# A two-block transformer step on one core: first modulation rows in another order, shift added out of PSUM, constants and gains loaded in parts

## The reference, cut to what matters

```python
mod = silu(c) @ ada_w + ada_b                 # 9 rows of 1024: sh1, sc1, g1, sh2, sc2, g2, sh3, sc3, g3
y = rmsnorm(x, ffn1_pre_g) * (1 + sc1) + sh1
y = (silu(y @ w_gate) * (y @ w_up)) @ w_down  # 1024 -> 2816 -> 1024
h = x + 0.5 * g1 * rmsnorm(y, ffn1_post_g)
# then: a mixer of mLSTM and HGRN2 heads, a second FFN, a second block with
# attention, an RWKV recurrence and a retrieval over 16384 experts
```

## Time and profile before

| | us |
|---|---|
| median of 3 runs | 1949.12 (1948.37 to 1952.76) |
| the profiled execution | 1958.65 |
| its span in the trace | 1956.8 |
| start of the first FFN matmul in it | 53.58 |
| TensorE busy in the span | 1811.9 (93%) |

### The profile page before, as it was taken

The page is one execution under the profiler, slowest core; times in us unless marked ns, Lnnn a source line. Parts: engine busy times, 40 slices in busy tenths (PEclk is TensorE's granted clock), DMA queues, the critical chain, the costliest instruction groups (busy, mean ns, idle before and its releaser), DMA issues.

```text
span 1956.8 us, 32839 instructions
## 1 busy us (share of the span) xinstructions
PE 1811.9 (93%) x12830; PEld 1557.4 (80%) x12830; DVE 1139.4 (58%) x1952; ACT 768.4 (39%) x1170; POOL 334.8 (17%) x314
## 2 busy tenths in 40 slices
PE   4999998987899999999878899999999999999997
PEld 1777877864399978976863798999999998888885
DVE  2443545759355544695443469958889964444444
ACT  2333344451345444552111443444444443333334
POOL 1000000000000000000000038760000025555553
PEclk8999997999999998999998899999999999999999
DMA  9566554521555553442003335554444456666664
GB/s 359 208 257 245 170 178 178 185 86 66 225 172 189 176 172 119 151 151 87 3 2 129 130 123 164 179 162 140 142 141 142 145 175 192 193 192 192 193 191 158
DMA packets 62080, 315.98 MB, mean 161 GB/s; under 512 B 6896, under 2 KB 7184, under 8 KB 40720
## 3 DMA queue, kind: packets, MB, share of 16 engines
q1 hardware_dynamic: 60768, 305.94, 46.8%
q10 hardware_dynamic: 1136, 8.39, 1.2%
q0 software_dynamic: 64, 0.04, 0.0%
HBM read 313.29 MB, written 1.05 MB: 161 GB/s over the span
## 4 chain that ended last, share of the span: by engine, by line
PE 76%; DVE 9%; DMA 7%; ACT 4%; POOL 2%; issue 2%; SPq 0%; POOLq 0%; DVEq 0%; ACTq 0%
PE bank L375 21%; PE bank L376 20%; PE bank L377 20%; DMA ring<-in_stream 4%; PE bank L590 3%; DMA ring<-in_experts 2%; PE bank L2127 2%; DVE ring_rounded L353 2%; POOL ring_rounded L2419 2%; PE bank L536 2%; ACT arena_rounded L342 1%; PE bank L641 1%; DVE field L1320 1%; ACT ring_rounded L2225 1%; PE bank L1549 1%
## 5 line engine op out<-in xcount | busy, mean ns | idle before, releaser
L377 PE MATMUL bank<-yb_rounded,ring_rounded 128*128 128x256 f32 x2080 | 595.3, 286 | 0.0
L377 PEld LDWEIGHTS bank<-yb_rounded,ring_rounded 128*128 128x128 f32 x2080 | 406.0, 195 | 0.0
L353 DVE TENSOR_TENSOR ring_rounded<-ring,arena_rounded 128x1024 fp32r<-128x1024 f32 x218 | 256.9, 1221 | 218.7 <-ACT arena_rounded L342 218.4
L2225 ACT CAST ring_rounded<-ring 128x1024 fp32r<-128x1024 f32 x250 | 262.6, 1051 | 279.1 <-DMA ring<-in_experts 279.1
L375 PE MATMUL bank<-yb_rounded,arena_rounded 128*128 128x256 f32 x1104 | 323.5, 293 | 24.1 <-POOL ring_rounded L831 10.2
L376 PE MATMUL bank<-yT_rounded,arena_rounded 128*128 128x256 f32 x1104 | 319.7, 290 | 0.0
L342 ACT CAST arena_rounded<-ring 128x1024 fp32r<-128x1024 f32 x222 | 221.3, 1047 | 191.3 <-PE bank L375 119.6
L375 PE MATMUL bank<-yb_rounded,ring_rounded 128*128 128x256 f32 x976 | 283.0, 290 | 10.3 <-POOL ring_rounded L2419 7.9
L376 PE MATMUL bank<-yT_rounded,ring_rounded 128*128 128x256 f32 x976 | 275.9, 283 | 0.0
L2378 DVE TENSOR_TENSOR ring_rounded<-ring,ring_rounded 128x1024 fp32r<-128x1024 f32 x128 | 156.9, 1226 | 191.6 <-ACT ring_rounded L2225 191.6
L376 PE MATMUL bank<-ring_rounded,arena_rounded 128*128 128x512 f32 x688 | 268.4, 390 | 0.0
(11 more groups left out here) (389 smaller groups left out, 2606.1 us busy)
## 6 DMA issues: line engine op xcount, KB each, us to landing
ring<-in_stream SPq DMA_DIRECT2D x160, 1024.0 KB, 4.9
ring<-in_experts SPq DMA_DIRECT2D x256, 512.0 KB, 3.5
field<-in_gains ACTq DMA_DIRECT2D x1, 2560.0 KB, 8.9
const<-in_const SPq DMA_DIRECT2D x1, 1602.0 KB, 15.1
field<-in_gains ACTq DMA_DIRECT2D x1, 1536.0 KB, 6.7
xh<-in_x ACTq DMA_DIRECT2D x1, 1024.0 KB, 5.5
field<-in_norms ACTq DMA_DIRECT2D x1, 1024.0 KB, 10.3
field<-in_lns ACTq DMA_DIRECT2D x1, 1024.0 KB, 4.7
```

The source lines that it names most:

```text
L353: ins = nc.vector.tensor_tensor(ring_r[:, g % SLOTS, half], ring[:, g % SLOTS, half], top.bitcast(F32), ALU.subtract)
L377: return first, pe.matmul(bank, s_rest, m_top, start=False, stop=stop)
L2225: nc.scalar.copy(expert_top[:, n % E_SLOTS, :], expert_w[:, n % E_SLOTS, :]).then_inc(expert_top_ready, 1)
```

## The change

The row tiles are made in the order 2, 3, 0, 1 (`sc1` ahead of `sh1`). The bias matmul of a tile comes first in its bank, ahead of the wait for the tile's first chunk. The sum of a tile is issued between the two chunks of the next. DVE forms the scale row and multiplies both halves of the tokens while the shift tiles are computed. The sums of the shift tiles go to a `V` bank, and DVE adds them from there, times 1/32, to the 512 columns of each token half. Each such piece (two per column half) is transposed at once. Both transposes of the first column half stand in TensorE's queue ahead of the last row chunk. The ACT copies and DVE subtractions of the pieces are interleaved to match, with DVE's split of the first FFN chunk behind the last shift piece. SP loads 256 columns of `const` at the beginning and the rest ahead of chunk 20, the fourth round's first FFN tile. The load of five gain rows becomes two on ACT's queue, one row after round g = 1 and four rows after round g = 3.

```diff
+        V_seen, V_end, chunk_at, split_base = {}, {}, {"ffn1": 2 * 4}, {}
         silu_c = tiny[:, 0:KT * 32].rearrange("p (k n) -> p k n", k=KT)
         ADA, ADA_FIRST = N_MOD * D // 512, 4
+        FIRST_ROWS = [2, 3, 0, 1]
...
+        def first_rows_pe(pe, bank, tile, c):
+            if c == 0:
+                pe.matmul(bank[0:32, :], ones_32, arena1[:, tile * 512:(tile + 1) * 512], start=True, stop=False)
+            w = next_chunk(pe)[:, :].rearrange("p (k n) -> p k n", k=4)
+            for k in range(4):
+                ins = pe.matmul(bank[32 * k:32 * k + 32, :], silu_c[:, 4 * c + k, :], w[:, k, :],
+                                start=(c == 0 and k > 0), stop=(c == 1))
+                if k == 0:
+                    ins.then_inc(begun, 1)
+            if c == 1:
+                ins.then_inc(A.done, 1)
+        def first_sum_pe(pe, bank, tile, queue=A):
+            pe.matmul(bank[:, :], cst("ones"), partial(tile), start=True, stop=True).then_inc(queue.done, 1)
+        def first_turn_pe(pe, bank, i):
+            t, k = i % 2, i // 2 * 4
+            pe.wait_ge(sem("y_ffn1"), i + 1)
+            for j in range(4):
+                ins = pe.transpose(bank[:, j * P:(j + 1) * P], yb[:, t, (k + j) * P:(k + j + 1) * P], ident)
+            ins.then_inc(V.done, 1)
...
-            if tile in (0, ADA_FIRST):
-                pe.wait_ge(sem(f"ada_b_in{int(tile > 0)}"), 16)
+            if tile == ADA_FIRST:
+                pe.wait_ge(sem("ada_b_in1"), 16)
...
         def ada_pe(pe):
             pe.wait_ge(sem("silu_c_spread"), 1)
-            for tile in range(ADA_FIRST):
-                ada_groups_pe(pe, tile)
-                if tile == 0:
-                    pe.wait_ge(sem("const_in"), 16)
-                else:
-                    ada_sum_pe(pe, tile - 1, but=1)
-            ada_sum_pe(pe, ADA_FIRST - 1)
+            pe.wait_ge(sem("ada_b_in0"), 16)
+            sc_a, sc_b, sh_a, sh_b = FIRST_ROWS
+            rows = A.take(pe)
+            first_rows_pe(pe, rows, sc_a, 0)
+            first_rows_pe(pe, rows, sc_a, 1)
+            pe.wait_ge(sem("const_in"), 16)
+            for last, tile in ((sc_a, sc_b), (sc_b, sh_a)):
+                total, rows = A.take(pe), A.take(pe)
+                first_rows_pe(pe, rows, tile, 0)
+                A.evacuated_but(pe, 2)
+                first_sum_pe(pe, total, last)
+                first_rows_pe(pe, rows, tile, 1)
+            rows = A.take(pe)
+            first_rows_pe(pe, rows, sh_b, 0)
+            A.evacuated_but(pe, 1)
+            first_sum_pe(pe, V.take(pe), sh_a, V)
+            for i in range(2):
+                first_turn_pe(pe, V.take(pe), i)
+            first_rows_pe(pe, rows, sh_b, 1)
+            A.evacuated(pe)
+            first_sum_pe(pe, V.take(pe), sh_b, V)
+            for i in range(2, 4):
+                first_turn_pe(pe, V.take(pe), i)
+            V.evacuated(pe)
+        def first_turn_act(act, i):
+            t, k = i % 2, i // 2 * 4
+            act.wait_ge(V.done, FIRST_TURNS[i] + 1)
+            bank = V.banks[FIRST_TURNS[i] % 4]
+            nc.scalar.copy(y_top[:, t, k:k + 4, :], bank[:, :].rearrange("p (j s) -> p j s", j=4)
+                           ).then_inc(sem("y_top_ready"), 1)
...
-            for tile in range(ADA_FIRST):
+            for tile in FIRST_ROWS[:2]:
                 ada_groups_act(act, tile)
-                if tile:
-                    ada_sum_act(act, tile - 1)
-            ada_sum_act(act, ADA_FIRST - 1)
-            marks["first_rows"] = (A.free, 4 + A.emptied.n)
+                ada_sum_act(act, tile)
+                mark(f"row{tile}", A.free, 4 + A.emptied.n)
+            ada_groups_act(act, FIRST_ROWS[2])
+            for i in range(2):
+                first_turn_act(act, i)
+            ada_groups_act(act, FIRST_ROWS[3])
+            first_top_act(act, "ffn", "ffn1")
+            for i in range(2, 4):
+                first_turn_act(act, i)
...
-            dve.wait_ge(*marks["first_rows"])
             dve.wait_ge(sem("first_gain_in"), 16)
-            v(nc.vector.scalar_tensor_tensor(mod[:, SC1, :], mod[:, SC1, :], 1.0, gains[:, 0, :], ALU.add, ALU.mult))
+            for n, tile in enumerate(FIRST_ROWS[:2]):
+                at = slice(n * 512, (n + 1) * 512)
+                await_mark(dve, f"row{tile}")
+                ins = nc.vector.scalar_tensor_tensor(mod[:, SC1, at], mod[:, SC1, at], 1.0, gains[:, 0, at], ALU.add, ALU.mult)
+            v(ins)
+            for t in range(TT):
+                scaled_dve(t, SC1)
+            for n in range(2):
+                bank = V.get(dve)
+                at = slice(n * 512, (n + 1) * 512)
+                for t in range(TT):
+                    ins = nc.vector.scalar_tensor_tensor(yb[:, t, at], bank[:, :], 1.0 / 32, yb[:, t, at], ALU.mult, ALU.add
+                                                         ).then_inc(sem("y_ffn1"), 1)
+                dve.wait_ge(sem("y_ffn1"), 2 * n + 2)
+                nc.vector.memset(small[:, 510:511], 0.0).then_inc(V.free, 1)
+                if n == 1:
+                    first_rest_dve(dve, "ffn", "ffn1")
+                for i in (2 * n, 2 * n + 1):
+                    first_turn_dve(dve, i)
...
+        def first_turn_dve(dve, i):
+            t, k = i % 2, i // 2 * 4
+            turns.n += 1
+            dve.wait_ge(sem("y_top_ready"), turns.n)
+            bank = V.get(dve)
+            nc.vector.tensor_tensor(y_rest[:, t, k:k + 4, :], bank[:, :].rearrange("p (j s) -> p j s", j=4),
+                                    y_top[:, t, k:k + 4, :].bitcast(F32), ALU.subtract).then_inc(V.free, 1)
...
-            dve.wait_ge(sem("gains_in"), 16)
+            dve.wait_ge(sem("gains_in"), 32)
...
-            turn_pe(pe, yb, tag)
-            A.evacuated(pe)
+            if tag == "ffn2":
+                turn_pe(pe, yb, tag)
+                A.evacuated(pe)
...
-            if tag == "ffn1":
-                first_top_act(act, "ffn", tag)
-            turn_split_act(act)
+            if tag == "ffn2":
+                turn_split_act(act)
...
+                    if g == 1:
+                        act.dma_start(arena2[:, D:2 * D], dram["gains"][D:2 * D].partition_broadcast(P)).then_inc(sem("gains_in"), 16)
+                    if g == 3:
+                        act.dma_start(arena2[:, 2 * D:6 * D], dram["gains"][2 * D:6 * D].partition_broadcast(P)
+                                      ).then_inc(sem("gains_in"), 16)
...
-            if tag == "ffn1":
-                first_rest_dve(dve, "ffn", tag)
-                for t in range(TT):
-                    scaled_dve(t, sc)
-                    shifted_dve(t, sh, tag)
-            else:
+            if tag == "ffn2":
                 after_first_rest_dve("ffn", tag)
-            turn_split_dve(dve, turned_at[tag])
+                turn_split_dve(dve, turned_at[tag])
...
+            pe.wait_ge(sem("masks_in"), 16)
...
+            dve.wait_ge(sem("masks_in"), 16)
...
-        source = tile_at(range(ADA_FIRST))
+        source = tile_at(FIRST_ROWS)
...
-                    sp.dma_start(const[:, :], dram["const"]).then_inc(sem("const_in"), 16)
+                    sp.dma_start(const[:, 0:2 * P], dram["const"][:, 0:2 * P]).then_inc(sem("const_in"), 16)
 
             for g in range(SLOTS, stream.shape[0]):
+                if g == 20:
+                    sp.dma_start(const[:, 2 * P:], dram["const"][:, 2 * P:]).then_inc(sem("masks_in"), 16)
                 sp.wait_ge(begun, g - 2)
                 sp.dma_start(ring[:, g % SLOTS, :], stream[source[g]]).then_inc(landed[g % SLOTS], 16)
...
-            act.dma_start(arena2[:, D:6 * D], dram["gains"][D:6 * D].partition_broadcast(P)).then_inc(sem("gains_in"), 16)
             ffn_act(act, "ffn1")
```

More of the change, by code:

```diff
@@ L698, in ada_dve @@
             ins.then_inc(sem("silu_c_spread"), 1)
-            dve.wait_ge(*marks["first_rows"])
             dve.wait_ge(sem("first_gain_in"), 16)
-            v(nc.vector.scalar_tensor_tensor(mod[:, SC1, :], mod[:, SC1, :], 1.0, gains[:, 0, :], ALU.add, ALU.mult))
+            for n, tile in enumerate(FIRST_ROWS[:2]):
[17 more added lines that the diff above has]
+                    first_turn_dve(dve, i)
+        FIRST_TURNS = [1, 2, 4, 5]
+        def first_turn_dve(dve, i):
[5 more added lines that the diff above has]
+                                    y_top[:, t, k:k + 4, :].bitcast(F32), ALU.subtract).then_inc(V.free, 1)
         def ada_behind_groups_pe(pe, where):
@@ L890, in ffn_act @@
                 bank_root_act(act, V_end[tag], 1, BY_TOKEN)
-        V_seen, V_end, chunk_at, split_base = {}, {}, {}, {}
         chunk_of = {"mix2": 2 * ADA + FT + FT // 2 + 6 + 10 + 4 + FT + FT // 2}
```

## The result

| | before | after |
|---|---|---|
| median of 6 runs, us | 1949.03 (1948.15 to 1954.29) | 1940.23 (1936.94 to 1943.58) |
| ratio | | 0.995, 95% interval 0.9934 to 0.9966 |
| profiled execution, us | 1958.65 | 1943.58 |
| its span | 1956.8 | 1941.3 |
| first FFN matmul | 53.58 | 38.35 |

The change saves 8.8 us by the medians, 0.45%. The forecast was 1937.3 with a range of 1932 to 1944.5. The windows of the changed kernel, to be read beside the earlier trace rows: us, busy (x) of TensorE, its weight loads, VectorE, ScalarE and GpSimd, granted clock, DMA share, GB/s. The beginning is 15.3 us shorter and its mean clock is 0.99 instead of 0.84. The second window is the third hosted pair.

A forecast was written before the change was run, and what follows sets the result against it. The prediction took transfers up to 33.50 us, then a serial chain to the first FFN matmul at 53.58, to bound the beginning. It took 13.3 - 1.5 = 11.8 us off 1949.1, giving 1937.3, range 1932 to 1944.5.

The forecast's parts named there:

- The net of 11.8: Whole kernel: 13.3 us won by the earlier FFN start, less 1.5 us for loads moved into the FFN.
- the prediction's own signs of being wrong: FFN start past 43, a chunk in the load-carrying pairs over 7 us to land, or a pair with clock at 0.50.
- Part 1: Beginning: fewer `const` bytes ahead of the last row chunk land it 3.8 us earlier, at 29.7.
- Part 2: Chain behind chunk 6: shift sum, pieces and turns end at 32.1; the last row chunk waits 2.4 us.
- Part 3: Chain behind chunk 7: 8.0 us at full clock, 9.8 at half; FFN start at 40.3, 13.3 us earlier.
- Part 4: First FFN pairs: moved gain and mask loads mostly fit 4.8 us idle DMA time per pair, costing 1.5 us.
- Rival B: FFN pairs: moved loads starve tiles, each microsecond costing two; full form 1956 (chance 0.05), mild form 1945.4 (0.07).
- A: Beginning: clock stays at 0.50, FFN starts at 45 to 47, time 1942 to 1944; chance 0.17.
- C: Beginning and FFN: landings at 28.3, full clock, loads free; 16.8 us gained, 1932.3; chance 0.11.
- D: Beginning: the small `const` lands late and TensorE waits before the second tile; no chance of its own.

The follow-up runs named there:

- the whole table: The changed kernel with all of `const` loaded in one load at its old place and no load ahead of chunk 20: 1944.82 us.
- all turns behind: The changed kernel with masks ahead of chunk 47, gains behind g = 8, and both column halves transposed after the last row chunk: 1936.13 us.
- the last chunk first: The changed kernel with masks ahead of chunk 47, gains behind g = 8, and the last row chunk's matmuls ahead of the first two turns: 1936.31 us.
- late-loads: The changed kernel with five gain rows in one load behind g = 8 and the masks ahead of chunk 47: 1936.76 us.
- masks alone: The changed kernel with five gain rows in one load behind g = 8 and only the masks left ahead of chunk 20: 1933.76 us.
- extra matmuls: The changed kernel with masks ahead of chunk 47, gains behind g = 8, and three unread matmuls behind the last turn: 1932.63 us.
- loads two rounds later: The changed kernel with masks ahead of chunk 28, one gain row behind g = 3 and four behind g = 5: 1939.35 us.
- all together: The changed kernel with masks ahead of chunk 47, gains behind g = 8, turns behind the last row chunk, four unread matmuls: 1933.68 us.

## Why the prediction was right, and which terms were off

**The sign** came out as forecast, and the time lies in the range. The net of 11.8 was 3.0 too much. It is a sum of two terms that were both mis-sized, in opposite ways: the start was 15.2 earlier and not 13.3, and the FFN gave back about 7.1 and not 1.5 (the balance is below). The first alone put right gives 1935.4, the second alone 1942.9; the range is wide enough for either. That the errors run against each other was luck, not reasoning. Of the prediction's own signs of being wrong, one appeared: the pair of chunk 20 shows the clock at 0.50, from about 92.2 to 95.6. A second, a chunk over 7 us, was missed by a hair (6.99 and 6.98).

**Part 1, bytes: 3.8 taken, 4.8 measured** (33.50 to 28.74 in the kernel with only the constants split; 4.7 the other way round, with the whole table). For the first chunks the bytes were right: with the constants split, chunks 2, 3 and 5 were each begun 3.5 earlier. Chunks 4, 6 and 7 were begun 4.0, 4.5 and 4.8 earlier. What the bytes left out: in the kernel before, TensorE at half clock began chunk 4 late, and SP issues chunk 7 by that. Its chain goes this way, from chunk 4's matmuls (25.72) to the transfer of chunk 7 (26.73, 6.73 us). No run isolates this link. In the kernels with this chunk ahead of the turns it was begun at 28.6, so it had landed 1.1 ahead of the 29.7 taken.

**Part 2: the order held, its times were short.** Chunk 6 was begun at 26.22 (27.1 forecast), a shift piece took 0.69 where 0.75 was taken. The last row chunk's matmuls began at 30.52 (32.1 forecast): 0.9 by chunk 6, the rest mostly by the turns, 1.22 together at full clock where 2.0 was taken. A wait of 2.4 for chunk 7 was forecast, and about 1.9 was measured; taking it out gave the start 0.2 with the halves interleaved and 0.6 with all turns behind.

**Part 3: start at 40.3 forecast, 38.35 measured,** outside the bounds of 38.7 to 41.9. The chain behind chunk 7 itself was right: 8.0 us at full clock were added up, 7.8 were measured. It began 1.6 earlier, by Parts 1 and 2, and I had expected a mixture of clocks. In fact every matmul and turn from about 14 to 35.5 ran at 1.00: eight transposes took 1.22 here, 1.98 before. From the Trainium skill (TensorE: Matmul & The Clock Gate, Part 4: PE-mode transpose) the prediction had drawn that the turns let the clock fall ahead of chunk 7. The 1.06 of chunk 7 shows that it did not, with real matmuls on both sides of the turns. The same page of the Trainium skill says that the full rate doesn't engage for transposes; here the turns ran at a granted clock of 1.00, eight in 1.22. Whether they count towards keeping it is open: with the last chunk first, TensorE idled for 1.2 us behind the first turns, and the last ones ran at 0.50. The split of DVE in the last place of the chain was forecast and was there.

**Part 4, the step that was wrong: loads moved into the FFN, 1.5 taken, 5.8 measured** (3.6 in the pair of chunk 20 and 2.1 in that of chunk 28, against 16.3). The prediction took a pair's whole idle share, 4.8 us, as one pot. The late-loads windows show that it is not: between chunk 19's end and chunk 20's data the engines rest for some 3.4 us, and the remainder lies behind chunk 20, where it helps nothing. That the loads cause the delay is shown by moving them. The gap fits one row alone (1.3 us, no delay), but not the sizes: masks and one row, 5.1 us, minus 3.4 are 1.7, and 2.3 was measured; the masks alone should be late by 0.4, and were by 1.6. So its size stays open in part.

The rest of the loss is the clock, in one pair only. TensorE was idle for 2.83 us ahead of the tile of chunk 20 and for 2.82 ahead of that of chunk 28. Behind the first the clock was 0.50 for some 3.4 us, which by half is 1.7; behind the second it stayed at 1.00. So one pair lost 3.6 for a delay of 2.3, the other 2.1 for 2.2. No run shows what decides between them. Rival B had the mechanism right, but "each microsecond costs two" was too much: it was 1.6 in one pair and 1.0 in the other. It needed 6.7 us of delay to turn the sign, and got about 4.5.

**The balance.** At the last hosted sum the changed kernel is 12.9 ahead. Of that, 4.8 are the slow pair of the profiled execution of before, so 8.1 are the change's, near the 8.8 of the medians. It adds up: 15.2 at the FFN's start; 14.3 at the first hosted sum (76.57 and 62.31), since the FFN now runs at half clock for 6.0 us at its start, before for 3.8; and 6.2 lost in the pairs against the mean of 16.37 of the undisturbed ones before, of which 5.6 in the two named and the rest in a third of 17.07.

**Rivals A, C and D.** A fell with the clock. Its sum was also slightly off: three times 1.6 to 2 us on top of 41.9 give 46.7 to 47.9 and not 45 to 47. C had the start and the clock in the beginning, but neither free loads nor a fast first FFN tile; both were there for the taking, as late loads and extra matmuls showed. D fell: behind the first tile TensorE waited 0.78 us for chunk 2's transfer, not for the table.

## What to carry to other kernels

Spare DMA share is worth nothing in the mean. Ask in which gap it lies, and which transfer, on which the next tile hangs, is asked for at the gap's end. In this kernel bulk loads did no harm that shows where each chunk is issued two tiles ahead, nor beside work that needs no chunk. Where TensorE waits a few microseconds for another engine ahead of a dense stage, matmuls whose result nobody reads can pay for themselves (1.7 us in the trace here). Ahead of building an overlap by halves, see which engine ends last: here DVE did, with either order of the turns.

## What was not expected of the hardware

**The clock's record misses the first stretch.** In the kernel before, the windows from 10 to 18 us read a granted clock of 1.00, yet eight matmuls of the row chunks at 10.18 and 12.60 took 1.93 each time. They take 1.94 at 0.50 and 1.06 at the full clock.

```profile
10.00:12.00 2.00, 1.82 (x8) 0.20 (x8) 0.13 (x1) 0.46 (x3) 0.39 (x1) 1.00 1.04 442
```

```profile
10.18 1.93 PE L641 MATMUL bank<-ring,tiny 128*32 128x512 f32 x8 [10.18 <-DVE tiny L697]
```

**Chunk 36 was slow in three of twelve profiles without any load beside it:** 7.05 in the kernel before, 7.03 with the whole table, 7.33 with the last chunk first, each at another time (160, 154, 145 us) but at the same chunk. Its pairs took 20.3 to 21.2. In those three stretches the rate dipped in a window of 2 us behind the start, to 258, 274 and 242 GB/s. The instruction queue moved one packet in each of them, but it did so in nine of the twelve profiles in the 8 us behind this chunk's issue, and with turns behind the chunk then took 5.08. So the packet alone doesn't explain it, and the cause stays open. It also clouds the reading of chunk 36 with loads two rounds later.

**The rest of the program scatters.** From the last hosted sum to the end, twelve profiles took 1748.2 to 1761.3 us. The kernels are alike there but for the late loads of some, and these lie at both ends (1748.2 with the last chunk first, 1761.3 with all together). So single times and even medians of a few runs differ by 3 us with no reason in the edit that the trace shows (masks alone at 1933.76 beside late loads at 1936.76), and the sums' places in the trace were the better measure.
